# Masking the backward scores in their PSUM bank and adding the two directions, in a two-layer hybrid block

## The reference

```python
    scores = jnp.einsum('bnihd,bnjhd->bnhij', q * jnp.exp(g - g_mid), k * jnp.exp(g_mid - g))
    mask = jnp.tril(jnp.ones((GLA_CHUNK, GLA_CHUNK), dtype=bool))
    scores = jnp.where(mask, scores, 0.0)
    o_intra = jnp.einsum('bnhij,bnjhv->bnihv', scores, v)
    o_inter = jnp.einsum('bnihd,nbhdv->bnihv', q * jnp.exp(g), s_start)
    return (o_intra + o_inter).reshape(b, l, h, dv), s_final
...
    o_f, s_f = gla_chunked(q, k, v, gf, s_f0)
    o_b, s_b = gla_chunked(flip(q), flip(k), flip(v), flip(gb), s_b0)
    o = o_f + flip(o_b)
    o = o * lax.rsqrt(jnp.mean(o * o, axis=-1, keepdims=True) + RMS_EPS)
```

## Time and profile before

| | |
|---|---|
| median of 3 runs | 1694.77 us (1689.54 to 1698.43) |
| the profiled execution | 1690.27 us, span 1688.4 us |
| granted TensorE clock, mean | 0.98 |
| PE, DVE, ACT, POOL busy | 1594.3, 725.4, 568.6, 615.3 us |
| attention stage of layer 0 (scores of tile 0 to the end of L1815 of tile 5) | 295.8 to 350.1 us |
| the same of layer 1 | 1187.9 to 1226.7 us |

### The profile page before, as it was taken

The page is one execution under the profiler, slowest core; times in us unless marked ns, Lnnn a source line. Parts: engine busy times, 40 slices in busy tenths (PEclk is TensorE's granted clock), DMA queues, the critical chain, the costliest instruction groups (busy, mean ns, idle before and its releaser), DMA issues.

```text
span 1688.4 us, 22324 instructions
## 1 busy us (share of the span) xinstructions
PE 1594.3 (94%) x8868; PEld 1321.6 (78%) x8868; DVE 725.4 (43%) x1109; ACT 568.6 (34%) x897; POOL 615.3 (36%) x317
## 2 busy tenths in 40 slices
PE   5999999999899999999998989999997999999995
PEld 1677877877689989998997667887873888888884
DVE  2610225845566515762365474045735221221235
ACT  3634212523634313441243255432514321221221
POOL 1422111234424524553255443322233444444442
PEclk9899999999999999999999999999998999999998
DMA  9444332135412212222123562121171332332321
GB/s 372 154 160 138 105 129 88 38 137 202 172 51 76 88 37 76 76 76 75 50 76 146 209 240 80 63 76 51 32 268 62 100 99 88 100 99 88 100 78 59
DMA packets 48220, 186.21 MB, mean 110 GB/s; under 512 B 5062, under 2 KB 8006, under 8 KB 40968
## 3 DMA queue, kind: packets, MB, share of 16 engines
q1 hardware_dynamic: 44028, 170.29, 29.8%
q10 hardware_dynamic: 4108, 14.75, 2.3%
HBM read 173.49 MB, written 11.53 MB: 110 GB/s over the span
## 4 chain that ended last, share of the span: by engine, by line
PE 82%; DVE 6%; issue 4%; ACT 3%; POOL 2%; DMA 1%; SPq 1%; DVEq 0%; ACTq 0%; POOLq 0%
PE A L909 57%; PE A L1146 7%; PE N L1146 4%; PE G L1146 4%; POOL w_lo L846 2%; PE G L1199 1%; DMA raw<-modw 1%; PE N L929 1%; DVE x L1938 1%; PE A L1048 1%; PE G L1014 1%; PE G L929 1%; DVE y L1937 1%; PE G L982 1%; PE N L998 1%
## 5 line engine op out<-in xcount | busy, mean ns | idle before, releaser
L846 POOL TENSOR_TENSOR w_lo<-raw,w_hi 128x1024 fp32r<-128x1024 f32 (+2 forms) x183 | 422.5, 2310 | 747.9 <-ACT w_hi L1222 747.9
L909 PE MATMUL A<-h_hi,w_hi 128*128 128x512 f32 (+1 forms) x1232 | 418.4, 371 | 28.9 <-DVE h_lo L1955 16.0
L909 PE MATMUL A<-h_hi,w_lo 128*128 128x512 f32 (+1 forms) x1232 | 410.3, 365 | 0.0
L909 PE MATMUL A<-h_lo,w_hi 128*128 128x512 f32 (+1 forms) x1232 | 409.6, 364 | 0.0
L1222 ACT ACTIVATE w_hi<-raw 128x1024 fp32r<-128x1024 f32 (+2 forms) x183 | 184.9, 1012 | 483.7 <-PE A L909 442.6
L909 PEld LDWEIGHTS A<-h_hi,w_hi 128*128 128x128 f32 x1232 | 218.2, 191 | 88.7 <-issue 27.4
L909 PEld LDWEIGHTS A<-h_hi,w_lo 128*128 128x128 f32 x1232 | 218.8, 191 | 37.3
L909 PEld LDWEIGHTS A<-h_lo,w_hi 128*128 128x128 f32 x1232 | 218.7, 191 | 35.7 <-issue 0.2
L909 PE MATMUL A<-g_hi,w_hi 128*128 128x512 f32 (+1 forms) x528 | 170.0, 361 | 2.1 <-DVE g_lo L1670 2.0
L909 PE MATMUL A<-g_lo,w_hi 128*128 128x512 f32 (+1 forms) x528 | 168.0, 358 | 0.0
L909 PE MATMUL A<-g_hi,w_lo 128*128 128x512 f32 (+1 forms) x528 | 168.0, 357 | 0.0
(11 more groups left out here) (258 smaller groups left out, 2319.8 us busy)
## 6 DMA issues: line engine op xcount, KB each, us to landing
raw<-stream SPq DMA_DIRECT2D x150, 512.0 KB, 3.6
mraw<-modw SPq DMA_DIRECT2D x38, 1024.0 KB, 5.6
x<-x_keep ACTq DMA_DIRECT2D x6, 1536.0 KB, 10.1
raw<-pairs SPq DMA_DIRECT2D x18, 512.0 KB, 4.7
raw<-stream SPq DMA_DIRECT2D x24, 384.0 KB, 3.2
raw<-modw SPq DMA_DIRECT2D x6, 1024.0 KB, 14.7
mraw<-pairs SPq DMA_DIRECT2D x9, 512.0 KB, 3.6
x_keep<-x SPq DMA_DIRECT2D x4, 768.0 KB, 22.4
```

What stands on the lines that cost most here:

```text
L846: pool.tensor_tensor(w_lo[:, n % RING, 0:WIDTH[n]], raw[:, n % RAW, 0:WIDTH[n]], w_hi[:, n % RING, 0:WIDTH[n]].bitcast(F32), ALU.subtract) ...
L909: m = pe.matmul(dst[:, t0:t1], a, b[:, k, t0:t1], start=(first and p == 0), stop=(last and p == 2))
```

## The change

The forward scores are masked into Pm as before, but Pm now has one copy and one direction. The backward scores are masked where they lie in N: a tile of zeros, `none`, is copied over the places where the (now inverted) mask says so. After a link, two additions sum both directions into the new Ps, and only they free N. The output multiplies Ps with the values once per head, in place of Pm of each direction.

```diff
-                Pm = sb("Pm", [P, 2, 2, 2, 2, P], stack=late)
+                Pm = sb("Pm", [P, 2, 2, P], stack=late)
+                Ps = sb("Ps", [P, 2, 2, 2, P], stack=late)
+                none = sb("none", [P, 1, P], stack=late)
...
                     for pr in range(2):
-                        for g in range(2):
-                            for hp in range(2):
-                                h = 2 * pr + hp
-                                pe.matmul(o_at(b, h), vtok[:, tt, h * DV:(h + 1) * DV], Pm[:, b, hp, g, pr, :],
-                                          start=(g == 0), stop=False)
+                        for hp in range(2):
+                            h = 2 * pr + hp
+                            pe.matmul(o_at(b, h), vtok[:, tt, h * DV:(h + 1) * DV], Ps[:, b, hp, pr, :],
+                                      start=True, stop=False)
...
-                        link(dve.memset(Pm[:, :, :, :, :, :], 0.0))
+                        link(dve.memset(none[:, :, :], 0.0))
+                        link(dve.memset(Pm[:, :, :, :], 0.0))
...
+                    N4 = N[:, :].rearrange("p (q g r t) -> p q g r t", q=2, g=2, r=2)
                     for hp in range(2):
-                        for g in range(2):
-                            m = dve.copy_predicated(Pm[:, b, hp, g, :, :],
-                                                    mask[:, g:g + 1, :].to_broadcast([P, 2, P]),
-                                                    N[:, hp * 512 + g * 256:hp * 512 + (g + 1) * 256].rearrange("p (r t) -> p r t", r=2))
-                        m.then_inc(free[f"N{hp}"], 1)
+                        dve.copy_predicated(Pm[:, hp, :, :], mask[:, 0:1, :].to_broadcast([P, 2, P]), N4[:, hp, 0, :, :])
+                        m = dve.copy_predicated(N4[:, hp, 1, :, :], mask[:, 1:2, :].to_broadcast([P, 2, P]),
+                                                none[:, :, :].to_broadcast([P, 2, P]))
+                    link(m)
+                    for hp in range(2):
+                        dve.tensor_tensor(Ps[:, b, hp, :, :], N4[:, hp, 1, :, :], Pm[:, hp, :, :],
+                                          ALU.add).then_inc(free[f"N{hp}"], 1)
...
-    masks = np.stack([before, after], 1).astype(np.int32)
+    masks = np.stack([before, ~after], 1).astype(np.int32)
```

## The result

| | before | after |
|---|---|---|
| median | 1692.96 us (1689.54 to 1698.43, 4 runs) | 1711.66 us (1711.56 to 1712.81, 4 runs) |
| the profiled execution | 1690.27 us | 1711.77 us, span 1710.0 us |
| granted TensorE clock, mean | 0.98 | 0.965 |
| stage of layer 0 (first scores to the end of the last low part) | 54.3 us | 68.4 us |
| the same of layer 1 | 38.9 us | 46.8 us |

The ratio is 1.0115, 95% interval 1.0095 to 1.0136: 19.5 us slower (0.0115 times 1692), where the forecast was 10.7 and the top of the range stood 17.2 us above the kernel before. In the profiled executions the two stages are 21.9 us longer, which is the whole difference of 21.5; what lies between and behind them takes the same time as before to within 0.2 us.

What follows compares the result with a forecast made beforehand. Middle tiles were taken as paced by ACT, then POOL, then DVE, at 8.27 us, not by PE. Layer 0's 7.1 and layer 1's 3.6 us sum to 10.7: 1701.0 us profiled, 1705.5 as median; range 1693 to 1712.

Steps and rivals of the forecast that it cites:

- PE's output, 1.06 us shorter, on the path only at the ends: PE, each tile's output: half the matmuls saves 1.06 us, 10.6 over ten tiles, but nothing in middle tiles.
- Memsets worth nothing: Start of each layer: one 1.77 us memset gives way to two small ones and two links; no gain.
- DVE 0.8 us a tile, PSUM writes free: DVE, each tile: two additions 0.67 us and a link 0.115, together 0.8; masked copies into PSUM cost nothing extra.
- The fourth copy waits for POOL: DVE, middle tiles: second backward copy, both inputs in SBUF, ends 0.29 us after POOL; tile 9.4 us for 8.27.
- Its sum, 7.1 and 3.6 us: Added time of the layer 0 and layer 1 stages from the wait, additions and shorter output; total 10.7 us.
- the second tile of layer 0: Copies wait for POOL's two L874, so ACT's L1418 starts near 313.55 for 311.62: +1.95 us.
- the first round of layer 1: Layer 1's start: POOL's L874 end 0.6 us earlier, yet ACT's L1418 comes at 1203.3 for 1202.56: +0.7 us.
- last tile and end: End of layer 0's stage: output starts 2.84 us later and is 1.06 shorter; layer 1: +2.83 and -1.06.
- The clock: Rival 2: PE's clock falls to 0.50 in gaps before outputs, at most 7 us more, 1712 us; chance 0.12.
- Rival 1: Masked copies on DVE don't wait for POOL, rounds stay 8.27 us: total -0.5 us, 1694.3; chance 0.20.
- Rival 3: Middle tiles: the fourth copy is let in before POOL, second tile keeps its 1.95: about +3 us, 1698; chance 0.04.
- Rival 4: PE's saving reaches the end in first and last tiles and layer 1's second: five tiles, 5.3 us; chance 0.02.

Runs made afterwards that it cites:

- the kernel with the product: Kernel after the change, backward scores masked in N by a product with a mask of ones and zeros, not the copy of zeros: 1695.55 us, ratio 1.0020.
- the run with the clock held: Kernel after the change, useless matmuls on PE before each output except a layer's first, copies still waiting for POOL: 1704.19 us, ratio 1.0073.
- the kernel with the halved output: Kernel before the change, backward half of the output's products left out, DVE, ACT and POOL unchanged: 1692.19 us, ratio 1.0004.
- three kernels without the wait for POOL: Backward output products left out; product masking; sum by one product and one masked copy; each with useless matmuls on PE. Ratios to kernel before: 0.9957, 0.9978, 0.9956.

## Why the prediction was right in direction and wrong in size

- **PE's output, 1.06 us shorter, on the path only at the ends.** Right: from the first output matmul to the next scores it is now 3.23 us (329.33 to 332.56), the middle rounds didn't gain from it, and with the clock held 3.4 us came out at the ends.
- **Memsets worth nothing.** Right: 0.17 and 0.48 us, and the first scores start at 295.78 as before.
- **DVE 0.8 us a tile, PSUM writes free.** Right. In the kernel with the product, L1799 to L1789 is 321.12 to 323.26, 2.14 us; less four steps of 0.335 that is 0.80. The link shows there as 0.47 us between starts for 0.335, so 0.13. The page "VectorE: DVE Perf Modes" of the Trainium skill (The DRAIN you can't avoid), which measured a semaphore between copies to cost nothing extra, again differs from the trace. The copy into PSUM starts 0.33 us after its forerunner (325.15 after 324.82), and the next one 0.34 after it, like the others.
- **The fourth copy waits for POOL.** Right, to a hundredth: 2.50 us, ending 0.29 behind POOL, rounds of 9.39 and 9.38 for 9.40. One of the readings behind it was empty, though. The 22 rows of L1916 do not lie beside POOL's work: POOL runs there for 2.4 us in every 5.4 or so, and each L1916 falls into a pause (one from 1315.85 to 1316.54, POOL from 1311.53 to 1313.93 and from 1316.99). That one input in PSUM spares the wait is shown by the old masked copy at 313.89 and by the product, not by them. The Trainium skill's page "SBUF — State Buffer" (Who interferes with whom) gives the rule for any Vector instruction with two SBUF inputs, and these rows now show it for a masked copy; with one input in PSUM the same place takes 0.43.
- **Its sum, 7.1 and 3.6 us.** Near, as the run with the clock held shows: 6.9 and 4.2. That the total of 11.0 is so close to 10.7 is partly luck: the second tile of layer 0 was put 0.34 too high, the first round of layer 1 0.47 too low. By terms in layer 0: second tile +1.61 (313.64 less 296.21, for 15.82) where 1.95 stood, three rounds +3.4 as forecast, last tile and end +1.88 where 1.78 stood. In layer 1 the first tile gave +1.17 for 0.7: POOL's two L876 did not end 0.6 earlier but 10.97 us after the first scores, where they had ended at 10.92. One round gave 1.13 and the end +1.86 for 1.77.
- **The clock. This is the step that failed.** The text treated the lower clock as a rival with a chance of 0.12, held against the forecast. It is no rival to the wait but comes with it: the same 1.1 us that each round grows by are idle time of PE, and so are the 1.06 us a tile that it no longer works. The shorter output alone (20 us at 0.50) and the change without the wait (14) brought falls too, with the wait it was 47. The forecast itself counted 2.4 us of idle time before each output and then priced it at nothing. The term was worth 7 us by the ratios and 10.9 by the stages, and belonged in the sum. All that the text had for a clock that stays up was one stretch that kept 1.00, with 1.8 us of standing still in it; no row of it showed what longer waits, or one in every tile, would do.
- **The size inside the rival, "0.6 in each of some six tiles and 1.7 in two last ones".** Its total of 7 is at the low end of what was measured, but it was put in the wrong places. Most middle tiles had no fall. The two tiles behind a first fall cost 0.9 us each (rounds of 10.34 and 10.26), and the ends of the stages cost 6.2 and 2.9 more than with the clock held: near the end nearly all of PE's work is on the path (output, scores, mean of squares: 16.0 us of layer 0's chain from 338.71 on), not the output alone, and in layer 0 the clock stayed at 0.50 over 22 us, not over one output. Its price for an output was too low as well: the last one ran wholly at 0.50 and took 6.2 us (350.54 to 356.7), 2.95 more than the 3.23 at 1.00, where the text has 1.7.
- **Rival 1.** Its mechanism is what the kernel with the product does (wait on the first product, rounds unchanged). It was priced at -0.5; that kernel measured +3.4, and with the clock held -1.7 by the ratios and -0.2 by the stages, against the kernel before with its clock held at the ends. Again the clock was what the sum lacked.
- **Rival 3** did not come about: 0.14 us behind POOL was late enough for the wait, as L1788 in the earlier trace rows had said with 0.10.
- **Rival 4** had rightly almost no chance (0.02), and for a reason beside the one given: even without any cost on DVE, PE's saving brought nothing (1.0004) until PE was kept busy.

What stays open: by the stages of the profiled executions the clock's part is 10.9 us, by the ratios 7. The two intervals leave the 7 uncertain by 4 to 5. Every profiled execution also has stretches at 0.50 outside the two stages, at places that differ somewhat from kernel to kernel, and single profiles can't average these out. Which gap brings the clock down was not settled either: it fell behind a wait of 1.12 us in one kernel and not behind one of 2.25 in another.

## What to carry to other kernels

Before costing a change that shortens PE's work or lengthens its waits, draw PE's timeline of the stage as it will be, with its waits, and where it will stand still for longer or more often than the trace shows at 1.00, put the price of half the clock into the sum itself: 0.8 of the time of all that PE then has on the path (1.97 us for 1.11). A matmul saved in a stage that others pace is not free of effect: it can cost the clock, and a few useless matmuls in the gap can be what makes the saving pay. And look at the memory of both inputs of a Vector instruction beside GpSimd's work: a mask and a tile of zeros in SBUF made a copy six times as long, a product with a mask against PSUM did not.

## What was not expected of the hardware

- PE's clock fell to the 1.2 GHz level in layer 0's stage, in which PE stood still for 3 us at most: with 1.97 us busy out of five (305 to 310), and after a wait of 2.25 us (338.71) and one of 1.67 us (336.96 in the kernel with the halved output). An equal wait of 2.25 us one round earlier (329.33) brought no fall, and in the kernel with the product the clock fell during an output that had waited only 1.12 us (331.81).
- Three useless matmuls (0.83 us) before each middle output, one before the last and five in one gap of 1.7 us were enough, with the eight at the stage's end, to have 1.00 through the stage of layer 0 in three kernels without the wait for POOL; without the five, the clock of the last of the three kernels still fell near the end (0.50 at 338 to 340).
- A wait of DVE for POOL moves with the instruction that stands there: the same four copies cost 8.5 us less when the two with both inputs in SBUF came first (1.0065 for 1.0115).
